# Opening phase of a two-layer transformer step: three weight chunks in order of K, the first modulation in eight stages

## What is computed

```python
mod = silu(cond) @ w_ada[l] + b_ada[l]              # cond: two vectors of 2048, w_ada[l]: 2048 x 6144
shift, scale, gate = split(mod, 3)
h = rmsnorm(x, norm_pre[l]) * (1 + scale) + shift   # 384 x 2048
proj = h @ w_in[l]                                  # 2048 x 5120
# layer 0: q, k, v, g_a, u_b, g_b -> windowed attention with sink | 2-D DFT mixing, each times silu(gate path)
# layer 1: u_c, g_c, u_d, v_d, g_d -> pooling | chunked spatial gating, each times silu(gate path)
x = x + gate * rmsnorm(concat(...) @ w_out[l], norm_post[l])   # w_out: 2048 x 2048
```

## Time and profile before

| | us |
|---|---|
| median of 3 runs | 1242.26 |
| lowest, highest | 1241.4, 1242.9 |
| the profiled execution, its own time | 1244.44 |
| its span | 1242.6 |
| PE busy in the span | 1172.8 |
| DVE busy | 525.7 |
| ACT busy | 407.0 |

### The profile page before, as it was taken

One profiled execution on the slowest core, in us unless ns is written; L12 is line 12 of the kernel. 1 busy time (PEld: TensorE's weight loads), 2 busy tenths in 40 slices (PEclk: granted clock), 3 DMA queues, 4 the chain that ended last, 5 costly groups with the idle time before them and its releaser, 6 DMA issues.

```text
span 1242.6 us, 14007 instructions
## 1 busy us (share of the span) xinstructions
PE 1172.8 (94%) x5692; PEld 887.8 (71%) x5692; DVE 525.7 (42%) x826; ACT 407.0 (33%) x623; POOL 16.5 (1%) x33
## 2 busy tenths in 40 slices
PE   3788999999999999999999699999999999999995
PEld 0445577777777877777777377788888888888873
DVE  1644543454454452243323574325534433343333
ACT  2322222333354433233222454222343222333331
POOL 0000100000000000010000000000000000000000
PEclk9999999999999999999999899999999999999998
DMA  9988936435444556458566727454433433334412
GB/s 353 332 299 300 326 127 248 158 140 227 148 172 171 209 197 237 141 196 316 187 228 237 300 75 269 155 197 156 136 118 120 136 125 115 133 102 136 136 34 102
DMA packets 89807, 232.80 MB, mean 187 GB/s; under 512 B 4192, under 2 KB 4224, under 8 KB 81168
## 3 DMA queue, kind: packets, MB, share of 16 engines
q1 hardware_dynamic: 86976, 221.26, 49.6%
q0 software_dynamic: 2192, 7.49, 1.8%
q10 hardware_dynamic: 576, 3.16, 0.6%
HBM read 228.23 MB, written 3.67 MB: 187 GB/s over the span
## 4 chain that ended last, share of the span: by engine, by line
PE 89%; DVE 4%; DMA 3%; ACT 2%; issue 1%; DVEq 0%; SPq 0%; ACTq 0%
PE bank L595 25%; PE bank L597 24%; PE bank L596 24%; PE bank L569 4%; DMA raw_first<-in_w_ada 3%; PE bank L616 2%; PE bank L697 1%; DVE x L1022 1%; DVE silu L1127 1%; PE bank L680 1%; PE bank L652 1%; DMA raw<-in_w_ada 1%; PE bank L742 1%; DVE h_op L1131 1%; ACT h_op L840 1%
## 5 line engine op out<-in xcount | busy, mean ns | idle before, releaser
L595 PE MATMUL bank<-w_hi,h_op 128*128 128x512 f32 x1152 | 474.4, 412 | 10.0 <-DVE h_op L1131 9.9
L597 PE MATMUL bank<-w_hi,h_op 128*128 128x512 f32 x1152 | 453.5, 394 | 0.0
L596 PE MATMUL bank<-w_lo,h_op 128*128 128x512 f32 x1152 | 453.2, 393 | 0.0
L977 DVE TENSOR_TENSOR w_lo<-raw,w_hi 128x1024 fp32r<-128x1024 f32 x224 | 272.1, 1222 | 266.0 <-ACT w_hi L779 265.5
L779 ACT ACTIVATE w_hi<-raw 128x1024 fp32r<-128x1024 f32 x224 | 234.9, 1054 | 242.0 <-PE bank L597 242.0
L595 PEld LDWEIGHTS bank<-w_hi,h_op 128*128 128x128 f32 x1152 | 218.5, 190 | 89.6 <-issue 46.5
L597 PEld LDWEIGHTS bank<-w_hi,h_op 128*128 128x128 f32 x1152 | 218.3, 190 | 48.0
L596 PEld LDWEIGHTS bank<-w_lo,h_op 128*128 128x128 f32 x1152 | 219.0, 190 | 41.4 <-issue 0.7
L595 PE MATMUL bank<-w_hi,o_low 128*128 128x512 f32 x192 | 76.2, 397 | 0.0
L597 PE MATMUL bank<-w_hi,o_low 128*128 128x512 f32 x192 | 74.9, 390 | 0.0
L596 PE MATMUL bank<-w_lo,o_low 128*128 128x512 f32 x192 | 74.9, 390 | 0.0
(11 more groups left out here) (158 smaller groups left out, 710.3 us busy)
## 6 DMA issues: line engine op xcount, KB each, us to landing
raw<-in_w_in SPq DMA_DIRECT2D x80, 1024.0 KB, 5.1
raw<-in_w_ada SPq DMA_DIRECT2D x64, 1024.0 KB, 8.7
raw_first<-in_w_ada SPq DMA_DIRECT2D x32, 1024.0 KB, 7.9
raw<-in_w_out SPq DMA_DIRECT2D x32, 1024.0 KB, 5.0
x<-in_x_sample ACTq DMA_DIRECT2D x2, 1024.0 KB, 14.3
out_y_sample<-x SPq DMA_DIRECT2D x8, 256.0 KB, 3.1
x<-in_x_prompt ACTq DMA_DIRECT2D x1, 1024.0 KB, 9.4
bias_rows<-in_ada_rows POOLq DMA_DIRECT2D x4, 256.0 KB, 2.9
```

The costliest lines, as they stand in the source:

```text
L595: pe.matmul(out, operand(layer, kind, 0, k, t), hi, start=k == 0, stop=False)
L596: pe.matmul(out, operand(layer, kind, 0, k, t), lo, start=False, stop=False)
L597: last = pe.matmul(out, operand(layer, kind, 1, k, t), hi, start=False, stop=k == KT - 1)
L977: dve.tensor_tensor(w_lo[:, half % WRING, :, :].rearrange("p k n -> p (k n)"), src, hi, ALU.subtract)\
```

## The change

- The opening takes three chunks (v, k, the first q) in order of K. `HALVES` lists their 24 halves; from chunk 3 on all is as before. Chunk 0 keeps its sums in banks 0 to 2. Chunks 1 and 2 share banks 3 to 5: each is summed over 4 k-steps only, then DVE adds the three banks to `partial` in SBUF (`spill`, 24 operations of 128x512), and PE waits for that before the other chunk's next group (`wait_spilled`). k and q are rotated out of `partial`, `new_k` is stored from there.
- `partial` lies over the first tile and half of the second of x. So x is loaded first of all, on SP's queue, is normed into `mixed`, and ACT loads two of its tiles again at chunk 5 (`reload`). The square sum of the second tile moves from ACT to DVE (`square`).
- The first modulation has eight stages of 256 columns, for scale and shift at once, each with four `first_ada(b, i)` of 1 MB. Such a load is two DMAs of 512 KB, in pieces of 1 KB where pieces of 2 KB were. Each stage ends with one `first_cols` and gives two K tiles. Their sums alternate between `rows` and `gate`.
- `h`: ACT writes scale and shift once, in float32, into `h_full` (two tiles in `silu`), frees the side bank and rounds from there with a third activation. DVE only subtracts. This goes for both layers.
- The `ada` pairs of layer 0's time start at chunk 3, 7.2 k-steps apart instead of 8, and end at chunk 13 as before. `cols` of the scale stands four k-steps later in chunk 10.

```diff
+FIRST = 3
+STAGES = 8
+KEPT, SPILLED = 0, (1, 2)
+HALVES = [half for q in range(4) for half in (
+    [(1, 0), (0, 0), (1, 1), (0, 1), (2, 0), (2, 1)] if q == 0 else
+    [(0, 2 * q), (1, 2 * q), (1, 2 * q + 1), (0, 2 * q + 1), (2, 2 * q), (2, 2 * q + 1)])]
+HALVES += [(c, h) for c in range(FIRST, len(CHUNKS)) for h in range(KT // 2)]
...
+def bank_set(c):
+
+    return (c > 0) if c < FIRST else (c + 1) % 2
...
+    steps = [(c, 2 * h + i) for c, h in HALVES[:FIRST * KT // 2] for i in range(2)]
+
+    def first(n, *entry):
+        put(*steps[n], *entry)
+
+    pre(0, "square")
+    for i in range(4):
+        pre(0, "first_ada", 0, i)
+        if i == 1:
+            pre(0, "norm")
+    pre(0, "first_weights")
+    pre(0, "first_cols", 0)
+    for k in range(2):
+        pre(0, "h", 0, k)
+    for i, n in enumerate((0, 1, 2, 2)):
+        first(n, "first_ada", 1, i)
+    first(3, "first_cols", 1)
+    for k in range(2, 4):
+        first(3, "h", 0, k)
+    for b in range(2, STAGES):
+        at_ = 12 * (b // 2 - 1) + 4
+        ada, cols, h = ((0, 1, 2, 4), 5, 6) if b % 2 == 0 else ((5, 6, 7, 8), 9, 10)
+        for i in range(4):
+            first(at_ + ada[i], "first_ada", b, i)
+        first(at_ + cols, "first_cols", b)
+        for k in range(2 * b, 2 * b + 2):
+            first(at_ + h, "h", 0, k)
+    for c in SPILLED:
+        for q in range(4):
+            for t in range(TOKS):
+                put(c, 4 * q + 3, "spill", c, q, t)
...
-        if c == 0:
+        if c == KEPT:
 
...
-        put(2 + n // 2, 8 * (n % 2) + 5, "ada", m, k, 2)
+        put(FIRST, 5 + 36 * n // 10 * 2, "ada", m, k, 2)
...
-    put(10, 1, "cols", SCALE_BLOCK)
+    put(10, 5, "cols", SCALE_BLOCK)
...
+        if p[0] == "at" and p[2] % 2 == 0:
+            n = NTH_HALF[p[1], p[2] // 2] + (3 if p[1] < FIRST else 2)
+            if n < len(HALVES):
+                c, h = HALVES[n]
+                if n == min(NTH_HALF[c, h // 2 * 2 + i] for i in range(2)) and NTH_QUARTER[c, h // 2] == fetched:
+                    loads.append(("mm", fetched))
...
+        partial = tensor("partial", [2, TOKS, CW], at=place[0])
...
+            for t in range(TOKS):
+                src = x_prompt[0] if t == 0 else x_sample[0, (t - 1) * P:t * P, :]
+                sp.dma_start(x[:, t, :], src).then_inc(x_in[t], 16)
...
+                    b, i = what[1:]
+                    for w, third in enumerate((SCALE_COL, SHIFT_COL)):
+                        col = third * D + b * 2 * P
+                        sp.dma_start(
+                            raw_first[:, n % FIRST_RAW, :].rearrange("p (k w n) -> p k w n", k=4, w=2)[:, :, w, :],
+                            w_ada[0].rearrange("(k p) n -> p k n", p=P)[:, 4 * i:4 * i + 4, col:col + 2 * P])\
+                            .then_inc(first_raw_in[n % FIRST_RAW], 16)
...
+                if c in SPILLED and k % 4 == 0 and half:
+
+                    if c == SPILLED[1]:
+                        wait_spilled(pe, SPILLED[0], k // 4, TOKS - 1)
+                    else:
+                        wait_spilled(pe, SPILLED[1], k // 4 - 1, TOKS - 1)
...
+                group = 4 if c in SPILLED else KT
                 for t in range(TOKS):
                     out = acc(c, t)[:, :]
-                    pe.matmul(out, operand(layer, kind, 0, k, t), hi, start=k == 0, stop=False)
+                    pe.matmul(out, operand(layer, kind, 0, k, t), hi, start=k % group == 0, stop=False)
                     pe.matmul(out, operand(layer, kind, 0, k, t), lo, start=False, stop=False)
-                    last = pe.matmul(out, operand(layer, kind, 1, k, t), hi, start=False, stop=k == KT - 1)
+                    last = pe.matmul(out, operand(layer, kind, 1, k, t), hi, start=False,
+                                     stop=k % group == group - 1)
...
+                    full = h_full[k % 2]
                     for c_, lo_, hi_ in ((0, 0, P), (1, P, NT)):
-                        last = act.activation(h_op[:, 0, k, lo_:hi_], side_bank(e)[:, lo_:hi_], ACT.Identity,
+                        last = act.activation(full[:, lo_:hi_], side_bank(e)[:, lo_:hi_], ACT.Identity,
                                               bias=shift_t[:, k, c_:c_ + 1], scale=scale_t[:, k, c_:c_ + 1])
-                    last.then_inc(op_hi, 1)
+                    freed(last, e)
+                    wait_free(act, *e)
+                    act.activation(h_op[:, 0, k, :], full, ACT.Copy).then_inc(op_hi, 1)
...
+                elif what == "reload":
+
+                    act.wait_ge(roped_ready, nth_roped[SPILLED[1], TOKS - 1] + 1)
+                    wait_full(act, "turn", SPILLED[1], 0)
+                    act.wait_ge(k_stored, 16)
+                    for t in range(2):
+                        act.dma_start(x[:, t, :], x_prompt[0] if t == 0 else x_sample[0, 0:P, :]).then_inc(x_again, 16)
...
+                if what == "square":
+                    dve.wait_ge(x_in[1], 16)
+                    dve.scalar_tensor_tensor(out=mixed[:, 1, :], in0=x[:, 1, :], scalar=1.0, in1=x[:, 1, :],
+                                             op0=ALU.mult, op1=ALU.mult, accum_out=stat[:, 4, 1:2])\
+                        .then_inc(own_squared, 1)
+                elif what == "spill":
+                    c, q, t = e[1:]
+                    part_ = partial[:, c - 1, t, :]
+                    dve.wait_ge(mm_done, NTH_HALF[c, 2 * q + 1] + 1)
+                    if q == 0:
+                        dve.tensor_copy(part_, acc(c, t)[:, :]).then_inc(spilled, 1)
+                    else:
+                        wait_spilled(dve, c, q - 1, t)
+                        dve.tensor_tensor(part_, acc(c, t)[:, :], part_, ALU.add).then_inc(spilled, 1)
...
-                    for c_, lo_, hi_ in ((0, 0, P), (1, P, NT)):
-                        last = dve.tensor_scalar(h_tmp[:, lo_:hi_], side_bank(e)[:, lo_:hi_],
-                                                 scale_t[:, k, c_:c_ + 1], shift_t[:, k, c_:c_ + 1],
-                                                 ALU.mult, ALU.add)
-                    then_own(last)
-                    freed(dve.tensor_tensor(h_op[:, 1, k, :], h_tmp, h_op[:, 0, k, :].bitcast(F32), ALU.subtract), e)
+                    dve.tensor_tensor(h_op[:, 1, k, :], h_full[k % 2], h_op[:, 0, k, :].bitcast(F32), ALU.subtract)\
+                        .then_inc(h_ready, 1)
```

255 lines of the change are left out of this document (131 added, 124 removed).

## The result

The changed kernel takes **1227.3 us** (median of 4 runs, 1224.5 to 1227.8) where the kernel before takes 1242.1 (4 runs beside them): a ratio of **0.988** [0.986, 0.989] (the 95% interval in brackets, here and below). The forecast was 1228.5. The profiled execution took 1227.19 us with a span of 1225.4; before, these were 1244.44 and 1242.6.

What follows compares the result with a forecast made beforehand. PE bounds the kernel, with time to win only in the opening and at the seam. Gains of 13.1 us in the opening and 0.7 at the seam, 13.8 from 1242.26, gave 1228.5 us; forecast band 1224 to 1233, range 1221 to 1242.

Steps and rivals of the forecast that it cites:

- The start: Opening up to the first k-step: the second `w_in` load decides, first k-step at 35.9 us, 8.3 us earlier.
- The ruler: Priced PE work from first k-step to chunk 3: 143.2 us, 151.4 with losses; 0.3% off on the kernel before.
- Stage 1: Opening, after the fourth k-step: a PE wait of 2.5 us, then a half-clock stretch costing 1.6 us.
- Even stages: Stages 2, 4, 6 of the opening: next `first_ada` waits for the side bank, 0.75 us each, 2.2 in all.
- Odd stages: Stages 3, 5, 7 of the opening: 2.44 us of cover against a 2.4 us `h` chain, 0.3 us for three.
- Spills: Opening, banks 3 to 5: 6 us or more between groups against 3.8 us of copies, so no cost.
- The `ada` pairs: Two pairs move from the opening into chunks 3 to 13, where PE pays their 4.2 us; denser spacing costs nothing.
- The seam: Between the layers: shorter `h` chain, first k-step of layer 1 at 715.6 instead of 716.34, 0.7 us gained.
- A: Odd stages of the opening: covers too short, up to 4.0 us a stage, 1240 us; chance 0.14.
- B: Opening: smaller loads make it DMA-bound and slower, 1265 us if one fixed part shows per load; chance 0.07.
- C: Behind the opening: denser `ada` pairs give time back, landing waits of 1 to 2 us, 1233 to 1240; chance 0.07.
- D: Better than forecast: no slow stretch at stage 1, free 1 KB pieces, seam gain doubled, 1225 us; chance 0.10.

Runs made afterwards that it cites:

- e4: The changed kernel with x loaded on ACT's queue beside SP's loads, as before, instead of at the head of SP's queue: 1226.3 us.
- e5: The changed kernel with each first-modulation load as one 1 MB DMA in 2 KB pieces, shift columns left out, same amount of work: 1224.5 us.
- e6: The changed kernel with each first-modulation load as four DMAs of 256 KB in pieces of 512 B: 1230.4 us.
- e8: The changed kernel with the second half of weights rounded and split behind the first two h tiles instead of ahead of the first columns: 1224.9 us.
- e7: The changed kernel with first_cols and the two h tiles of stage 1 at the third k-step instead of the fourth: 1225.3 us.
- e9: The changed kernel with the two h tiles of the even stages 2, 4 and 6 one k-step apart instead of together: 1225.9 us.
- e3: The changed kernel with the old h chain: ScalarE writes the high part, DVE computes h again and frees the side bank: 1238.9 us.
- e1: The changed kernel with two chunks (v, k) beside the loads instead of three, no spill, no reload, ada pairs where they stood before: 1238.2 us.
- e2: The kernel before with only the h part of the change: ScalarE writes h once and frees the side bank, DVE only subtracts: 1235.3 us.

## Why the prediction was right

- **The start** (forecast 35.9, measured 35.45). The stream's count of MB and the 9 ns a piece give the second `w_in` load at 30.4; ACT rounds it at 30.33. The chain of `h` took 2.20 us (33.25 to 35.45) and not 2.4, its copy 0.52 and not 0.51. e4 shows that x's queue does not matter, e5 and e6 the price of a piece on both sides, e8 that the second load decides.
- **The ruler.** The opening took 150.5 us from the first k-step. Less waits (2.1 + 2.2) it is 146.2. The slow clock at the first k-step cost 2.1 and not 1.6 (the k-step took 4.11 us where the ruler has 2.04), the one at stage 1 1.6; less both it is 142.5, where the sum of the work was 143.2. So the ruler is 0.5% too long.
- **Stage 1**: 2.5 and a slow stretch foreseen, 2.10 and a slow stretch found; that the stop comes from a cover one k-step short is shown by e7. **Even stages**: 0.75 foreseen, 0.73 found three times, removed by e9. **Odd stages**: 0.3 foreseen for the three; found is no wait that the view of waits names, and 0.05 each by the timeline. The chain is 2.21 long (90.85 to 93.06), and the cover ends where it does. **Spills**: nothing foreseen, nothing found; no wait of PE names `partial`.
- **The `ada` pairs**: here a term was mis-sized. I let the two moved pairs cost 4.2 us behind the opening. They cost 3.0: from 206 us to the start of chunk 13 PE's stops of over 0.25 us add up to 2.2 us where they were 3.2, and 1.0 of the 4.2 is that.
- **The seam**: 0.7 foreseen, 0.9 found, with the longer wait for the norm that the prediction named (3.35 to 5.16). A further 1.0 in chunk 14 I had at nothing: 0.5 of it is that the half clock ends 2.7 us behind its first k-step instead of 3.8, and 0.4 are two stops, of 0.26 and 0.18 us, that are gone.
- **The total.** By the profiled executions the gain is 17.2 us for a forecast of 13.8: 0.5 from the start, 0.7 from shorter waits and 0.7 from the ruler in the opening, less 0.5 for the slow clock at its start, 1.2 from the pairs, 1.2 from the seam and chunk 14, less 0.3 at the end. By medians it is 14.8. The forecast took its sum from a median that lay 2.2 us under the execution that it was measured in, and so part of the error does not show in the time. That the forecast lies 1.2 us from the measured time is in part luck: in the traces its gain is 3.4 us too small. Before's median was 1242.1 to 1244.0 in the five comparisons.

**The rivals.** A (covers too short): the cover of the odd stages held with nothing to spare, as A feared; with the longer chain of e3 each of them waits 0.34 us. B (the loads bind, slower): not with three chunks, where even at 3.60 us a load e6 waited 0.26 us; but e1 shows that the reasoning was sound, since with two chunks the same loads do bind. The prediction spoke of a third chunk as something that the loads must keep up with, and did not see that it is also what saves the change: the gain of the start would have been lost at 3.0 us a load, as e1 shows against e2. C (given back later): not seen. D: the slow stretch at stage 1 came, and e5 and e8 show that it need not have.

The Trainium skill, "DMA: Bandwidth & Descriptors", "Specifications", puts line rate at 512 B and more. The runs disagree: 1 MB takes 2.72 us in pieces of 2 KB, 3.00 at 1 KB and 3.60 at 512 B. Its section "Measured (HBM→SBUF, 128 partitions, SWDGE, issued from GpSimd)" wants transfers batched to 1 MiB or more; DMAs of 512 KB and 256 KB in a full queue showed no fixed part here beyond the 9 ns a piece.
